# Tiles of two picks x 64 tokens, column halves of TensorE, and a seventh slot for gathered rows

## What is computed

```python
def chunk(args):
    hc, ec, gc = args
    u_sel = jnp.take(u, ec, axis=0)
    act = jax.nn.gelu(jnp.einsum('chkd,cd->chk', u_sel, hc), approximate=False) * gc
    v_sel = jnp.take(v, ec, axis=0)
    return jnp.einsum('chk,chkd->cd', act, v_sel)
```

## Time and profile before

| | |
|---|---|
| median of 3 runs | 3600.69 us (3599.6 to 3603.47) |
| profiled execution, span from first to last instruction | 3601.5 us |
| its own device time | not listed apart; the span is 0.8 above the median |
| granted TensorE clock, mean | 0.970 |
| TensorE busy | 3316.3 us, 92% |
| VectorE busy | 2554.4 us, 71% |
| ScalarE busy | 1537.0 us, 43% |
| GpSimd busy | 770.5 us, 21% |
| DMA | 918.82 MB |

### The profile page before, as it was taken

One profiled execution on the slowest core, in us unless ns is written; L12 is line 12 of the kernel. 1 busy time (PEld: TensorE's weight loads), 2 busy tenths in 40 slices (PEclk: granted clock), 3 DMA queues, 4 the chain that ended last, 5 costly groups with the idle time before them and its releaser, 6 DMA issues.

```text
span 3601.5 us, 50492 instructions
## 1 busy us (share of the span) xinstructions
PE 3316.3 (92%) x18706; PEld 2633.5 (73%) x18706; DVE 2554.4 (71%) x4532; ACT 1537.0 (43%) x3089; POOL 770.5 (21%) x577
## 2 busy tenths in 40 slices
PE   7998889979898777799999999989999999999998
PEld 6886669855463222688777777767899988998898
DVE  6997143676777877687767777877867576768665
ACT  3222234245443333454444444545445443444443
POOL 1001236123435666122122122222200000000000
PEclk9999999999999999899899999999999999999999
DMA  3332224569999999699888899879956844453455
GB/s 123 94 95 75 75 83 141 182 272 397 407 415 421 417 411 418 261 377 389 324 321 312 305 372 385 317 296 341 374 176 188 267 141 131 133 184 106 140 184 156
DMA packets 184174, 918.82 MB, mean 255 GB/s; under 512 B 21536, under 2 KB 26912, under 8 KB 118128
## 3 DMA queue, kind: packets, MB, share of 16 engines
q0 software_dynamic: 73728, 536.90, 37.4%
q1 hardware_dynamic: 99248, 358.66, 29.9%
q10 hardware_dynamic: 10960, 20.12, 1.8%
HBM read 907.80 MB, written 7.80 MB: 254 GB/s over the span
## 4 chain that ended last, share of the span: by engine, by line
PE 72%; DVE 9%; DMA 7%; issue 5%; ACT 4%; POOL 2%; ACTq 0%; DVEq 0%; POOLq 0%
PE psum L715 54%; PE psum L1068 11%; DMA buffer_float<-in_peer_uv,buffer_uint 7%; DVE buffer_bfloat L2578 2%; POOL buffer_float L3259 2%; PE psum L1289 1%; ACT slabs_rounded L1452 1%; PE psum L723 1%; DVE buffer_float32r L2185 1%; PE psum L1274 1%; DVE norm_recip_root L2193 1%; DVE slabs_remainder L2279 1%; PE psum L1286 1%; PE psum L1372 1%; PE psum L1336 1%
## 5 line engine op out<-in xcount | busy, mean ns | idle before, releaser
L715 PE MATMUL psum<-buffer_float32r,slabs_rounded 128*128 128x256 f32 (+2 forms) x9568 | 2005.4, 309 | 70.3 <-POOL slabs_remainder L3244 30.1
L715 PEld LDWEIGHTS psum<-buffer_float32r,slabs_rounded 128*128 128x128 f32 x9568 | 1556.1, 192 | 217.3 <-issue 113.5
L715 PE MATMUL psum<-buffer_float32r,slabs_remainder 128*128 128x256 f32 (+2 forms) x4784 | 1439.8, 301 | 0.0
L2279 DVE TENSOR_TENSOR slabs_remainder<-raw_slabs,slabs_rounded 128x1024 fp32r<-128x1024 f32 x601 | 732.8, 1223 | 452.2 <-ACT slabs_rounded L1452 434.1
L1452 ACT ACTIVATE slabs_rounded<-raw_slabs 128x1024 fp32r<-128x1024 f32 x662 | 695.7, 1055 | 698.5 <-PE psum L715 620.7
L1068 PE MATMUL psum<-buffer_float,buffer_float 128*128 128x512 f32 x1712 | 825.2, 612 | 137.8 <-ACT buffer_float L1753 124.5
L715 PEld LDWEIGHTS psum<-buffer_float32r,slabs_remainder 128*128 128x128 f32 x4784 | 918.1, 192 | 29.8
L3259 POOL DMA_INDIRECT buffer_float<-in_peer_uv,buffer_uint x512 | 623.2, 1217 | 1330.8 <-PE psum L1068 753.6
L2578 DVE CUSTOM_DVE_ANT_0 buffer_bfloat<-buffer_float,buffer_float 128x1024 bf16<-128x1024 f32 x512 | 625.3, 1221 | 169.5 <-DMA buffer_float<-in_peer_uv,buffer_uint 160.8
L1068 PEld LDWEIGHTS psum<-buffer_float,buffer_float 128*128 128x128 f32 x1712 | 304.3, 193 | 519.6 <-issue 509.7
L1742 ACT ACTIVATE buffer_float<-buffer_float 128x1 f32<-128x1 f32 x512 | 100.3, 196 | 368.5 <-DVE buffer_float L2578 366.6
(11 more groups left out here) (213 smaller groups left out, 2039.0 us busy)
## 6 DMA issues: line engine op xcount, KB each, us to landing
raw_slabs<-in_slabs SPq DMA_DIRECT2D x682, 512.0 KB
buffer_float<-in_peer_uv,buffer_uint POOLq DMA_INDIRECT x512
buffer_float<-kept ACTq DMA_DIRECT2D x4, 874.5 KB, 6.0
xT<-in_xT ACTq DMA_DIRECT2D x4, 512.0 KB, 5.7
buffer_float<-in_consts ACTq DMA_DIRECT2D x8, 256.0 KB
kept<-buffer_float ACTq DMA_DIRECT2D x4, 512.0 KB
buffer_float<-kept ACTq DMA_DIRECT2D x2, 875.0 KB, 6.7
kept<-buffer_float ACTq DMA_DIRECT2D x4, 272.0 KB
```

Source lines behind the costliest of these rows:

```text
L715: m = pe.matmul(out, a, b, start=start and j == 0, stop=stop and j == 2)
L2279: dve.tensor_tensor(slab_l[:, r, :], raw[:, r, :], slab_h[:, j, :].bitcast(F32), ALU.subtract)\
```

## The change

- A tile is two picks of 64 tokens: still 128 gathered rows, of which rows 0 to 63 hold one pick of 64 tokens and rows 64 to 127 the next pick of the same tokens. There are 8 groups of 64 tokens with 64 tiles each, again n = 0 to 511.
- The diagonal becomes two 64 x 64 diagonals one above the other (`stacked`), 128x64. A matmul has 64 output rows; tile n goes to the lower or the upper 64 partitions of the bank, in turn (`j`). So the two halves of a bank hold two partial sums of the same tokens, and `turn_rows` adds them: it multiplies with `stacked` (8 matmuls, one bank) and no longer transposes.
- In the woven half two tiles are weighed together, their matmuls in turn, once both are due. In the pure half each is weighed by itself.
- `added_by` is `woven_by(t - 2)`, one slab sooner. A turn of the sums happens for each group: at t = 62, 117, 170 and 229. VectorE adds 80 of the 256 woven tiles itself.
- 7 slots. The dot product's products overwrite the `u` half in the slot, and `dot` waits for the previous one no more.
- A group's rows stand twice one above the other in `hrow`. For the first tile of tokens ScalarE copies them (`twin_rows`, eight copies). For the other three the rows are stored to DRAM (`rows_d`, 512 KB each), and each of six groups is loaded with two DMAs of 256 KB, issued by ScalarE.

```diff
@@ names
+H64 = P // 2
+GROUP = PICKS // 2
+GROUPS = 2 * QT
-SLOTS = 6
+SLOTS = 7
@@ when woven tiles are weighed
-def added_by(t, behind=3):
-
-    n = woven_by(t - behind)
-    return PICKS if n > PICKS and t < TURN[0] + 3 else n
+def held(n, t):
+
+    for bound, turn in zip(BOUNDS, TURN):
+        if n > bound and t < turn + 3:
+            return bound
+    return n
+
+
+def added_by(t, behind=2):
+
+    return held(woven_by(t - behind), t)
...
-    return n >= PURE and n % PICKS % 3 == 2
+    return n >= PURE and n % GROUP % 3 == 2 and n % GROUP < GROUP - 2
@@ TensorE
-            def weigh(n):
+            def weigh(*picks):
+
+                for n in picks:
+                    pe.wait_ge(uv_landed[n % SLOTS], 16 * (n // SLOTS) + 16)
+                pe.wait_ge(diag_done, DIAGONALS[picks[-1] + 1])
                 for q in range(2):
...
-                    m = pe.matmul(psum[:, b, :], diag[:, slot, :], uv_rows[slot][:, D + q * 512:D + (q + 1) * 512],
-                                  start=p == 0, stop=p == PICKS - 1)
+                    for n in picks:
+                        g, slot, j = n // GROUP, n % SLOTS, DIAGONALS[n] % 2
...
+                        m = pe.matmul(psum[j * H64:(j + 1) * H64, b, :], diag[:, slot, :],
+                                      uv_rows[slot][:, D + q * 512:D + (q + 1) * 512], start=first, stop=last)
...
+                for k in range(KT):
+                    m = pe.matmul(psum[:, bn[0], k * H64:(k + 1) * H64], out_rows[:, k * P:(k + 1) * P], stacked,
+                                  start=True, stop=True)
@@ ScalarE
+            def load_rows(g):
+
+                t, s = g // 2 - 1, g % 2
+                for c in range(2):
+                    act.dma_start(hrow[g][c * H64:(c + 1) * H64, :], rows_d[t, s * H64:(s + 1) * H64, :])\
+                        .then_inc(rows_here[s], 16)
...
-                act.activation(diag[:, slot, :], ident[:, :], ACT.Copy, scale=coefs[:, slot:slot + 1])\
+                act.activation(diag[:, slot, :], stacked, ACT.Copy, scale=coefs[:, slot:slot + 1])\
@@ VectorE
-                step(dve.tensor_copy(eidx[:, tt, h0 * TOPK:h1 * TOPK], pk.fin_af[:, some].rearrange("p a b -> p (a b)")))
+                two = pk.fin_af[:, some].rearrange("p h (i c) -> p c (h i)", c=2)
+                for s in range(2):
+                    for c in range(2):
+                        step(dve.tensor_copy(eidx[2 * tt + s][c * H64:(c + 1) * H64, h0 * TOPK // 2:h1 * TOPK // 2],
+                                             two[s * H64:(s + 1) * H64, c]))
...
-                if n:
-                    dve.wait_ge(dotted, n)
-                dve.tensor_tensor_reduce(dump, uv_rows[slot][:, 0:D], hrow[tt], 1.0, 0.0, ALU.mult, ALU.add,
+                dve.tensor_tensor_reduce(uv_rows[slot][:, 0:D], uv_rows[slot][:, 0:D], hrow[g], 1.0, 0.0, ALU.mult, ALU.add,
                                          dots[:, slot:slot + 1]).then_inc(dotted, 1)
```

More of the change, by code:

```diff
@@ L234 @@
     DIAGONALS.append(DIAGONALS[-1] + (not by_dve(_n)))
-assert not any(by_dve(tt * PICKS + p) for tt in range(QT) for p in (0, PICKS - 1))
+assert all(DIAGONALS[g * GROUP] % 2 == 0 for g in range(GROUPS + 1))
 def score_pieces(h):
@@ L620, in build @@
         picked = sem("peer_picked")
+        rows_made = sem("stream_rows_made")
+        rows_kept = sem("stream_rows_kept")
+        rows_here = [sem(f"stream_rows_here_{p}") for p in range(2)]
         uv_landed = [sem(f"uv_landed_{j}") for j in range(SLOTS)]
@@ L1091, in _ @@
                     next(steps)
-                if n == PICKS - 1:
-                    first_sums = list(sums_at)
-                if n == PICKS + 5:
-                    turn_rows(first_sums, [at.take(), at.take()])
+                if n % GROUP == GROUP - 1:
+                    last_sums = list(sums_at)
+                if n > GROUP and n % GROUP == TURN_AT:
+                    turn_rows(last_sums, at.take())
             assert next(steps, None) is None and slabs.value() == BLOCK1
-            turn_rows(list(sums_at), [at.take(), at.take()])
-            place, woven = [0], [0]
+            turn_rows(last_sums, at.take())
+            place, woven, waiting = [0], [0], []
             def weigh_to(n):
@@ L1104, in weigh_to @@
                     if not by_dve(PURE + woven[0]):
-                        weigh(PURE + woven[0])
+                        waiting.append(PURE + woven[0])
                     woven[0] += 1
+                    if len(waiting) == 2:
+                        weigh(*waiting)
+                        waiting.clear()
             def fill(behind=2):
@@ L1770, in _ @@
             turned = None
[L1771 to L1781 removed]
+            for n in range(PURE):
+                if n % GROUP == 0:
+                    sums = [acc.take(), acc.take()]
+                coefficient(n)
+                if n - STEP_LAG in STEPS:
+                    next(steps)
+                if n in GATE_PICK:
+                    gate_exps(GATE_PICK[n])
+                if n > GROUP and n % GROUP == TURN_AT + STEP_LAG:
+                    turned = at.take()
+                if n == LATE_ROWS:
+                    act.wait_ge(rows_kept, 16 * (QT - 1))
+                    load_rows(QT)
+                    load_rows(QT + 1)
+                if n % GROUP == GROUP - 1:
+                    take_sums(n // GROUP, sums, turned)
+            turned = at.take()
             assert next(steps, None) is None
@@ L2547, in make_gates @@
                 sync()
-                step(dve.tensor_tensor(gates[:, tt, :].rearrange("p (h k) -> p h k", h=PEER_HEADS),
-                                       pk.fin_e, pk.fin_r.unsqueeze(2).to_broadcast([P, PEER_HEADS, TOPK]), ALU.mult))
+                two = pk.fin_e.rearrange("p h (i c) -> p c h i", c=2)
+                by = pk.fin_r.unsqueeze(2).to_broadcast([P, PEER_HEADS, TOPK // 2])
+                for s in range(2):
+                    mine = slice(s * H64, (s + 1) * H64)
+                    for c in range(2):
+                        out = gates[2 * tt + s][c * H64:(c + 1) * H64, :].rearrange("p (h k) -> p h k", h=PEER_HEADS)
+                        step(dve.tensor_tensor(out, two[mine, c], by[mine], ALU.mult))
                 sync()
@@ L2739, in _, with add_sums @@
             last_row = [0]
-            def add_sums(tt, sums):
+            def add_sums(g, sums):
                 before = last_row[0]
```

206 lines of the change are left out of this document (107 added, 99 removed).

## The result

The changed kernel takes **3617.7 us** (median, 3613.6 to 3625.0) against 3601.3 for the kernel before on the same chip: a ratio of 1.0053, 95% interval 1.004 to 1.0067. I had forecast 3573. It is a small loss, 16 us and clear of the noise, inside the range of 3540 to 3625 and on the other side of zero. The profiled execution spans 3623.2 us, at a mean granted clock of 0.957.

The account below looks back on a forecast made before the run. The prediction took DMA to bound the pure half, and TensorE and DMA both to be near their bound in the woven half. Its terms summed to -30 from 3601.5, giving 3571 us, stated as 3573, range 3540 to 3625.

Parts of the forecast that it names:

- the rival of 3651: Woven half: the two column halves don't run together, so pairs cost +40 instead of -111; 3651 us, chance 0.14.
- the earlier trace gave 13.2: First feed-forward's down part: the late diagonal makes three slabs take 13.2 us instead of 11.71, +9 in all.
- the bound that I had set: Pure half: the forecast is wrong if the clock falls below 0.97 there because half the columns work.
- Mixer, 51 pairs: Mixer: raw saving -68, less DMA-bound pairs, four late-diagonal places (+15) and weighs already in gaps, leaving -39.
- slot, turn and extra-pick terms: Woven half: slots -4 and -2, two more turns +3, two row loads +1, four extra TensorE picks +4.
- The late diagonal eats it: Rival, woven half: TensorE waits about 1.3 us at most pairs, woven weighs gain 0; 3606 us, chance 0.12 including turns.
- Two of the signs that I had named: Mixer: some 35 us shorter, and its DMA share up from 0.87 to 0.92.
- Up part -4: First feed-forward's up part, 15 pairs: of raw -20 only -4 arrives, as DMA leaves 5% at best.
- The DMA isn't a wall: Rival, feed-forwards: at 409 GB/s up part -13 and second -10; 3557 us, or 3542 without attention stalls; no separate chance.
- Row loads +8: Pure half: two row stores and four loads, 3.15 MB at 409 GB/s on bound DMA engines, cost +7.7 us.
- Slots -6: Seven slots and two slabs behind: -4 at the turns of the sums, -2 at the first woven slabs.
- Second feed-forward -5: Second feed-forward, 13 pairs: of raw -17 only -5 arrives, as its steady DMA share is 1.00.

Follow-up runs that it names:

- e1: The changed kernel with woven tiles weighed three slabs behind instead of two, turns of the sums one slab later too: 3567.1 us, ratio 0.9912.
- e6: e1 with the row loads of groups 4 and 5 moved behind the pure half's last copy of sums: 3555.4 us, ratio 0.9878.
- e2: The changed kernel with woven tiles weighed one at a time instead of in pairs, still two slabs behind: 3686.7 us, ratio 1.0236.
- e3: The changed kernel without the row stores to DRAM and loads back, part of the result left wrong: 3597.3 us, ratio 0.9986.
- e4: The changed kernel with six gather slots instead of seven: 3630.4 us, ratio 1.0079.
- e5: The changed kernel with ScalarE's coefficients and diagonals put ahead of its rounding of the next slab: 3699.4 us, ratio 1.0281.
- e9: e6 with six gather slots instead of seven: 3604.2 us, ratio 1.0003.
- e11: e6 with woven tiles weighed four slabs behind instead of three, turns too: 3604.4 us, ratio 1.0011.
- e10: e6 with woven tiles two slabs behind in the first feed-forward's up part only, three from there on: 3562.8 us, ratio 0.9891.

## Why the prediction was wrong

**What held.** The halves run together: the pair costs 2.1 us, the work saved is 112 us, as worked out from the row halves and the narrow records, and the rival of 3651 is out. By the Trainium skill ("TensorE: Matmul & The Clock Gate", Part 3, what overlaps) weight loads pass matmuls in flight only when the row group differs, and the halves share all rows; the trace disagrees in so far as two such loads and passes take the time of one. The down part takes 13.6 us for three slabs, where the earlier trace rows gave 13.2, with TensorE waiting 2.35 to 2.38 at each pair there. That the figures are so near is partly luck: with a pair at full clock the loop takes 12.78, and the half clock, which no term had, adds the rest. That the row loads are not hidden and that the seventh slot helps held in sign. The mean clock of the pure half is 0.97, at the bound that I had set; TensorE has slack there, 555 us of work in 700.

**What failed** is the step "Mixer, 51 pairs": -68 raw, "four such places of 3 to 5 us: +15", left -39. It came out at +6 (with slot, turn and extra-pick terms in it that I had at +2 for the whole woven half). The size was not off by a little: I had counted a late diagonal only where one of my rows happened to show one. In the trace it is 45 pairs and 95.7 us over the woven half; in 1755 to 2475, the mixer, 57.9 us where it was 7.9. e1 undoes the lag alone and gets 30 us back in the mixer, by the profiled executions. So the rival "The late diagonal eats it" (3606) was the right one, at a chance of 0.12, and still too mild: it had 1.3 us at most pairs, measured are 2.1 us at half of them, and it had no half clock; what I had argued against it, that in the up part the chain holds TensorE alone, was read in the kernel with three slabs of lag, and says nothing on how much of that lag could be spared. Two of the signs that I had named failed with it: the mixer is 6 us longer and not 35 shorter, and its DMA share fell to 0.84. POOL's wait for a slot at the turn isn't gone either: at 2074.70 it is 11.70 us, where it was 13.04.

**The clock, which no term had.** The weigh at one place of the mixer, where ScalarE and VectorE work at a norm (start, us, idle before): before, a single pick; changed and e6, a pair:

```profile
2096.76 3.75 PE L1068 MATMUL psum<-buffer_float,buffer_float 128*128 128x512 f32 x4 [4.04 <-ACT buffer_float L1753]
```
```profile
2109.42 3.68 PE L1093 MATMUL psum<-buffer_float,buffer_float 128*64 128x512 f32 x8 [14.25 <-ACT buffer_float L1805]
```
```profile
2067.09 3.56 PE L1093 MATMUL psum<-buffer_float,buffer_float 128*64 128x512 f32 x8 [4.91 <-ACT buffer_float L1805]
```

Each runs at half clock behind its wait. I had listed this place among those where a weigh sits in a gap and costs nothing; two slabs behind, TensorE stands 14 us there. The diagonal isn't the first cause of this one. ScalarE had stood 12.74 us ahead of a rounding, by the profile for the landing of a store of the mixer, `kept` (its last piece, 32 KB, landed 13.0 us after its issue), where in e6 it stood 2.54 (changed, then e6):

```profile
2096.70 1.06 ACT L1479 ACTIVATE slabs_rounded<-raw_slabs 128x1024 fp32r<-128x1024 f32 x1 [12.74 <-DMA kept<-buffer_float]
```
```profile
2048.60 1.06 ACT L1479 ACTIVATE slabs_rounded<-raw_slabs 128x1024 fp32r<-128x1024 f32 x1 [2.54 <-DMA kept<-buffer_float]
```

The same wait is 11.8 us in e2, 11.6 in e3, 9.2 in e4 and 4.8 in e5, all with two slabs behind in the mixer, and at most 3.2 in the versions with more. The DMA share was 1.00 in the changed kernel while the store was under way (2083 to 2097), and 0.72 in e1 (2049 to 2053). That the full engines made it late fits this; no run separates it.

From 1480 to 2640 the granted clock was 0.50 for 83 us before, 143 in the changed kernel, 106 in e1 and e6, 147 in e9 and 181 in e11 (added up over the clock's record). TensorE doesn't work in all of it; up to slab 230 it costs 23 us more than before. Whether the clock would fall without the waits wasn't separated; in all traces the low stretches lie behind waits of TensorE, whatever it waited for.

**Smaller terms.** Up part -4: measured -13.6, so the wall of 397 GB/s that I took from the down part wasn't one there (the rival "The DMA isn't a wall" had -13). Two slabs behind, its pairs also wait, in the chain behind transfer, rounding and diagonal, and e10 against e6 puts 7 us on that (the changed kernel against e1: 2). Row loads +8: 14.5 in the pure half and 20 in all; I had counted bytes at the gathers' rate, and the lower rate of the slab queue in the earlier trace rows, which I had used for the upper end only, was the better guide, though 3.15 MB at 333 GB/s are 9.5 us and still short. Slots -6: about -13 (e4). Second feed-forward -5: -3. The turn in the down part (t = 62) and the stretch behind it: +5.9 between t = 62 and 68, in no term.

Put together, against the sum of -30: mixer +45 off, down part +11, pure half +3, up part -10, what follows t = 193 +4.5 (-2.8 + 2.3 against -5), less the +2 of the slot, turn and extra-pick terms, which lie in the stages; that is some +52, and -30 + 52 = +22, the difference of the two spans (3623.2 less 3601.5). The lag alone is 50.6 of it (e1). In the chances, "faster" at 0.64 and "slower" at 0.24 should have been 0.62 and 0.26 by their parts.

**How the slab of lag divides.** Between the changed kernel and e1 the stretch from slab 0 to slab 230 differs by 57.7 us: 40.5 of waits, 18.3 of half clock, and 1.1 more work in e1. These are one profiled execution each; the medians of the whole kernels differ by 50.6.

**Open.** How much of the half clock would be left without the waits, and what makes the store in the mixer late. An eighth slot beside four slabs of lag was not tried.

## What to carry to other kernels

Before shortening a hand-off by one step, measure at every place how much time it has to spare, not at those that already wait: for each consumer, the time from the producer's end to its use, less the time of the step that is taken away. Here one slab of lag was worth 50.6 us, and turned a gain of 34 into a loss of 16.

A faster piece of work on the busiest engine moves the bound to the ring around it. Then lag and buffers belong together: with the late row loads three slabs with seven slots gave 3555 us, three with six and four with seven 3604 both; without them three with seven gave 3567, two with seven 3618 and two with six 3630. Change them together and try the neighbours. And add up all waits of the busiest engine, not those for one producer: in e11 the waits for the diagonal had nearly gone, and the time was lost at others.

## What the runs showed of the hardware

- Two f32 matmuls on the two column halves of TensorE's array, with weight loads in twos, take the time of one: 0.43 us a pass of 512 columns at full clock. A visit to the narrow form costs about 0.3 us, alone (2.05 us for four passes, 1.72 in the wide form) or in pairs (2.06).
- Behind waits of TensorE at a pair the granted clock was often 0.50 and the passes 0.85 us apart, the pair 3.5 us long. It was no matter of the one wait's length: in the down part TensorE stood 2.35 to 2.38 us at each pair from 1674.68 to 1729.20, and every second one ran at half clock.
- With 4 KB packets among 8 KB ones, full DMA engines moved 374 GB/s, not 422, and the large packets' own rate fell from 416 to 379 (30 us each, e3 against the changed kernel).
- A store of 32 KB landed 13.0 us after its issue in the changed kernel, at a DMA share of 1.00 (2083 to 2097), and 2.8 us after it in e1, at 0.72 (2049 to 2053).
